# One edit in five parts to a two-layer hybrid trunk: filler and sine tables, first taps, inverse levels, row matmuls, paddings

## The reference

```
proj = hn @ w_in          # gdn qkv, z, beta, a; s5 u; lru x, y; ret q, k, v, g; gates
out_a = gated_deltanet(...)   # width-4 conv on qkv, chunks of 64, unit lower-triangular solve
out_b = s5_layer(...)         # 16 groups, 64 complex states each, diagonal scan
out_c = rg_lru_block(...)     # width-4 conv, gates, linear recurrence
out_d = retention(...)        # rotary q, k, decay, chunks of 128
merged = sum(gates * (branches @ w_branch));  x = x + merged @ w_out
```

## Time and profile before

| | us |
|---|---|
| median of 3 runs | 1408.02 (1407.67 to 1409.34) |
| profiled execution | 1406.48 |
| its span, first to last instruction | 1404.4 |
| TensorE busy | 1349.3 (96%) |
| VectorE busy | 928.1 (66%) |
| ScalarE busy | 645.9 (46%) |
| GpSimd busy | 352.5 (25%) |
| DMA queue's packets | 48.6% of 16 engines |
| mean granted TensorE clock | 0.994 |

### The profile page before, as it was taken

The page is one execution under the profiler, slowest core; times in us unless marked ns, Lnnn a source line. Parts: engine busy times, 40 slices in busy tenths (PEclk is TensorE's granted clock), DMA queues, the critical chain, the costliest instruction groups (busy, mean ns, idle before and its releaser), DMA issues.

```text
span 1404.4 us, 26420 instructions
## 1 busy us (share of the span) xinstructions
PE 1349.3 (96%) x11214; PEld 1317.5 (94%) x11214; DVE 928.1 (66%) x1339; ACT 645.9 (46%) x926; POOL 352.5 (25%) x235
## 2 busy tenths in 40 slices
PE   6999999999999999999999999989989999999998
PEld 6999999888898999999999999989888999999997
DVE  7777446886976855554477765578778677655544
ACT  6444546553234454443464454457332354544432
POOL 2000014355743720000110000235468254100000
PEclk9999999999999999999999999999999999999999
DMA  6555564443232545665555555455422335555553
GB/s 232 185 194 190 168 196 136 136 135 121 61 106 75 181 150 187 194 189 193 186 163 182 184 171 180 156 165 153 131 86 83 104 121 167 161 193 188 175 168 123
DMA packets 61316, 220.17 MB, mean 157 GB/s; under 512 B 6928, under 2 KB 7184, under 8 KB 60688
## 3 DMA queue, kind: packets, MB, share of 16 engines
q1 hardware_dynamic: 61200, 218.50, 48.6%
HBM read 217.42 MB, written 1.05 MB: 156 GB/s over the span
## 4 chain that ended last, share of the span: by engine, by line
PE 76%; DVE 14%; ACT 4%; issue 2%; POOL 2%; DMA 1%; SPq 0%; DVEq 0%; ACTq 0%; POOLq 0%
PE bank L479 23%; PE bank L481 22%; PE bank L480 22%; PE bank L731 2%; DVE wlo L1221 2%; ACT whi L893 1%; DVE qkv L1439 1%; PE bank L499 1%; PE bank L718 1%; DVE tmpA L1455 1%; DVE flat L1241 1%; POOL wlo L1130 1%; DMA raw<-weights 1%; DVE qkv L1437 1%; POOL big L1185 0%
## 5 line engine op out<-in xcount | busy, mean ns | idle before, releaser
L479 PE MATMUL bank<-xh,whi 128*128 128x256 f32 x2384 | 679.6, 285 | 11.4 <-DVE wlo L1221 7.8
L481 PE MATMUL bank<-xh,wlo 128*128 128x256 f32 x2384 | 665.3, 279 | 0.0
L480 PE MATMUL bank<-xl,whi 128*128 128x256 f32 x2384 | 664.7, 279 | 0.0
L1221 DVE TENSOR_TENSOR wlo<-raw,whi 128x1024 fp32r<-128x1024 f32 (+1 forms) x346 | 436.3, 1293 | 168.8 <-ACT whi L893 167.0
L893 ACT ACTIVATE whi<-raw 128x1024 fp32r<-128x1024 f32 (+1 forms) x414 | 415.3, 1036 | 121.4 <-DMA raw<-weights 89.7
L479 PEld LDWEIGHTS bank<-xh,whi 128*128 128x128 f32 x2384 | 449.6, 189 | 17.8 <-issue 8.8
L480 PEld LDWEIGHTS bank<-xl,whi 128*128 128x128 f32 x2384 | 450.6, 189 | 0.3
L481 PEld LDWEIGHTS bank<-xh,wlo 128*128 128x128 f32 x2384 | 450.3, 189 | 0.0
L1130 POOL TENSOR_TENSOR wlo<-raw,whi 128x1024 fp32r<-128x1024 f32 x68 | 172.8, 2553 | 197.2 <-ACT whi L893 197.1
L1171 POOL TENSOR_TENSOR flat<-flat 128x256 f32<-128x256 f32 x36 | 33.6, 933 | 729.7 <-ACT flat L912 728.7
L479 PE MATMUL bank<-hh,whi 128*128 128x256 f32 x704 | 198.9, 283 | 1.5 <-DVE wlo L1221 1.5
(11 more groups left out here) (347 smaller groups left out, 1420.4 us busy)
## 6 DMA issues: line engine op xcount, KB each, us to landing
raw<-weights SPq DMA_DIRECT2D x350, 512.0 KB, 4.0
raw<-weights SPq DMA_DIRECT2D x64, 448.0 KB, 3.9
cst<-consts SPq DMA_DIRECT2D x1, 1088.0 KB, 11.4
par<-params SPq DMA_DIRECT2D x1, 1072.5 KB, 7.7
par<-params SPq DMA_DIRECT2D x1, 1060.5 KB, 9.3
x<-x_in SPq DMA_DIRECT2D x1, 1024.0 KB, 5.4
y_out<-ret SPq DMA_DIRECT2D x4, 256.0 KB, 2.2
ropec<-positions SPq DMA_DIRECT2D x1, 128.0 KB, 2.1
```

The source lines that it names most:

```text
L479: mm(out, w[0], a[0], start=start, stop=False)
L480: mm(out, w[0], a[1], start=False, stop=False)
L481: return mm(out, w[1], a[0], start=False, stop=stop)
L1221: V.tensor_tensor(slot(wlo, i), slot(raw, i), r32(slot(whi, i)), ALU.subtract).then_inc(S("low_dve"), 1)
```

## The change

- The 14 filler matmuls behind the first piece of each down projection are taken out.
- The three table activations now have splits of pieces ahead of them: up to `dn1_0.2` ahead of the sine, up to `dn1_0.4` ahead of Abs, `dn1_0.5` ahead of the cosine.
- Tap 0 of both convolutions is made by ScalarE, 6 and 2 activations of 128x256, tied to VectorE by a new semaphore `taps`. The low parts under `ahead("su")` move from behind the last pass to behind the third.
- In each level of the inverse TensorE's order becomes t0, first half of the gate, xt0, ty0, t1, second half, xt1, ty1; `SIDE` follows, so the side banks are handed out in that order. ScalarE and VectorE make one piece for each pair instead of two ahead of both.
- The row matmuls contract over the 32 partitions that hold the row instead of 128.
- Paddings of 16 and 32 words ahead of `xh` and `xl` move all that lies behind them in SBUF: `xh` and `hh` by 64 bytes, `xl` and `hl` by 192.

```diff
@@ -154,8 +154,7 @@
          ("ktr", "dve"), ("vtr", "dve")]
         + [(n, "dve") for n in ("gb0", "gb1", "kk0", "bb0", "kk1", "bb1", "qk0", "qk1")]
         + [u for lv in range(LEVELS) for u in
-           ([(f"t0_{lv}", "act"), (f"t1_{lv}", "act")]
-            + [(f"{n}{hp}_{lv}", "dve") for hp in range(2) for n in LEVEL_UNITS[lv]]
+           ([u for hp in range(2) for u in [(f"t{hp}_{lv}", "act")] + [(f"{n}{hp}_{lv}", "dve") for n in LEVEL_UNITS[lv]]]
             + [(f"pq{s}", "dve") for s in ([2 * lv, 2 * lv + 1] if lv < 4 else [])]
             + ([("rotq", "dve"), ("rotk", "dve")] if lv == 4 else []))]
         + [("u", "act"), ("w", "act"),
@@ -234,6 +233,7 @@
         whi, wlo = sb("whi", SLOTS * SLOT, F32R), sb("wlo", SLOTS * SLOT, F32R)
         cst = sb("cst", NCST)
         par = sb("par", NPAR)
+        sb("before_xh", 16)
         xh = two("xh", KD, dt=F32R)
         wide = sb("wide", 32 * SEQ)[:].rearrange("p (k t) -> p k t", k=32)
         hh = two("hh", MF, dt=F32R, over="wide")
@@ -252,6 +252,7 @@
         flat8 = two("flat8", 8)
         brh = sb("brh", 8 * SEQ, F32R, over="flat8")[:].rearrange("p (n k t) -> p n k t", n=NB, k=2)
 
+        sb("before_xl", 32)
         xl = two("xl", KD, dt=F32R)
         big = sb("big", 24 * SEQ)
         hl = two("hl", MF, dt=F32R, over="big")
@@ -570,8 +571,6 @@
                             if (j, o, n) == (3, 1, 2):
                                 sum_of_first(which_after)
                             name = f"{unit}.{3 * o + n}"
-                            if (j, o, n) == (0, 0, 1):
-                                keep_busy(14)
                             wh, wl = piece(name)
                             for m in range(k0, k1):
                                 if j == 0 and o == 0:
@@ -641,7 +640,7 @@
             for t in range(2):
                 for hp in range(2):
                     h = 2 * t + hp
-                    last = mm(ps[64 * hp:64 * hp + 64, t * SEQ:(t + 1) * SEQ], ident[:, h:h + 1].to_broadcast([P, 64]), rows, start=True, stop=True)
+                    last = mm(ps[64 * hp:64 * hp + 64, t * SEQ:(t + 1) * SEQ], ident[0:32, h:h + 1].to_broadcast([32, 64]), rows[0:32], start=True, stop=True)
             last.then_inc(S("side"), 1)
             gate(0)
             pe.wait_ge(S("k_normed"), 1)
@@ -656,7 +655,7 @@
                 ps = side_bank(unit)
                 for t in range(2):
                     h = 2 * t + hp
-                    last = mm(ps[:, t * SEQ:(t + 1) * SEQ], ident[:, row + h:row + h + 1].to_broadcast([P, P]), rows, start=True, stop=True)
+                    last = mm(ps[:, t * SEQ:(t + 1) * SEQ], ident[row:row + 32, row + h:row + h + 1].to_broadcast([32, P]), rows[row:row + 32], start=True, stop=True)
                 last.then_inc(S("side"), 1)
 
             def against_k(unit, q0, hp):
@@ -717,8 +716,7 @@
                         else:
                             last = mm(ps[:, i * P:(i + 1) * P], lowc[:, hp, t, j, :], mx[:, hp, t, j, :], start=True, stop=True)
                     last.then_inc(S("side"), 1)
-                gate(4 + lv)
-                for hp in range(2):
+                    half(f"g{4 + lv}", hp)
                     if lv:
                         pe.wait_ge(S("side_act"), side.taken(f"t{hp}_{lv}"))
                     if lv > 1:
@@ -965,10 +963,13 @@
             A(sm["sn"], sm["r1"], ACT.Sin)
             A(sm["cs"], sm["r2"], ACT.Sin).then_inc(S("psin"), 1)
             silus(1, range(4, MF))
+            split_to(piece_at("dn1_0.2") + 1)
             act.wait_ge(S("turns"), 1)
             A(sinE, turns_b, ACT.Sin, scale=SIN_SCALE).then_inc(S("tables"), 1)
+            split_to(piece_at("dn1_0.4") + 1)
             act.wait_ge(S("tables"), 1)
             A(turns_b, turns_b, ACT.Abs).then_inc(S("tables"), 1)
+            split_to(piece_at("dn1_0.5") + 1)
             act.wait_ge(S("tables"), 2)
             A(cosE, turns_b, ACT.Sin, scale=-SIN_SCALE, bias=quarter_col).then_inc(S("tables"), 1)
             squares(0)
@@ -986,10 +987,18 @@
             split_to(piece_at("qkv2.0") + 1)
             A(tmpF[:, 1, :], tmpF[:, 0, :], ACT.Ln, bias=1.0).then_inc(S("ln1p"), 1)
             A(tmpB[:, 1, :], tmpB[:, 0, :], ACT.Tanh, scale=0.5).then_inc(S("ln1p"), 1)
+            def first_taps(i):
+                act.wait_ge(S("main_act"), main.taken(f"qkv{i}"))
+                for t in (2 * i, 2 * i + 1):
+                    last = A(qkv[:, t, :], qkvp[:, t, 0:SEQ], ACT.Identity, scale=par_("gconv", t, t + 1))
+                last.then_inc(S("taps"), 1)
+
             for i in range(3):
                 ahead(f"qkv{i}")
                 act.wait_ge(S("main"), main.ready(f"qkv{i}"))
                 A(qkvp[:, 2 * i:2 * i + 2, 3:], halves(main.bank(f"qkv{i}")[:]), ACT.Identity).then_inc(S("main_act"), 1)
+                if i:
+                    first_taps(i - 1)
             act.wait_ge(S("gc"), 1)
 
             A(tmpF[:, 0, :], tmpC[:, 0, :], ACT.Exp)
@@ -1003,7 +1012,12 @@
                 act.wait_ge(S("main"), main.ready(unit))
                 A(dst, halves(main.bank(unit)[:]), ACT.Identity).then_inc(S("main_act"), 1)
 
+            first_taps(2)
             copied("lx", lxp[:, :, 3:])
+            act.wait_ge(S("main_act"), main.taken("lx"))
+            for t in range(2):
+                last = A(tmpA[:, t, :], lxp[:, t, 0:SEQ], ACT.Identity, scale=par_("lconv", t, t + 1), bias=par_("lcb", t, t + 1))
+            last.then_inc(S("taps"), 1)
             copied("ly", ly)
             copied("su", su)
 
@@ -1070,6 +1084,7 @@
                 for hp in range(2):
                     act.wait_ge(S("side"), side.ready(f"t{hp}_{lv}"))
                     A(flat(mt if lv else mx)[:, hp, :], side.bank(f"t{hp}_{lv}")[:], ACT.Identity).then_inc(S("side_act"), 1)
+                    split_to(last_piece(f"g{4 + lv}") + 2 + hp)
                 gate(4 + lv)
             gate(10)
             act.wait_ge(S("s5gin"), 1)
@@ -1429,30 +1444,26 @@
             ahead("lx")
 
             gw = lambda k, t: par_("gconv", 6 * k + t, 6 * k + t + 1)
-            for k in range(4):
+            for k in range(1, 4):
                 for t in range(6):
-                    if k == 0:
-                        if t % 2 == 0:
-                            dve.wait_ge(S("main_act"), main.taken(f"qkv{t // 2}"))
-                        last = V.tensor_scalar(qkv[:, t, :], qkvp[:, t, 0:SEQ], gw(0, t), None, ALU.mult)
-                    else:
-                        last = V.scalar_tensor_tensor(qkv[:, t, :], qkvp[:, t, k:k + SEQ], gw(k, t), qkv[:, t, :], ALU.mult, ALU.add)
+                    if k == 1 and t % 2 == 0:
+                        dve.wait_ge(S("taps"), t // 2 + 1)
+                    last = V.scalar_tensor_tensor(qkv[:, t, :], qkvp[:, t, k:k + SEQ], gw(k, t), qkv[:, t, :], ALU.mult, ALU.add)
                 if k < 3:
                     link(last)
                 if k == 1:
                     ahead("ly")
+                if k == 2:
+                    ahead("su")
             last.then_inc(S("conv"), 1)
             ahead("su")
 
             xc = tmpA
-            dve.wait_ge(S("main_act"), main.taken("lx"))
+            dve.wait_ge(S("taps"), 4)
             lw = lambda k, t: par_("lconv", 2 * k + t, 2 * k + t + 1)
-            for k in range(4):
+            for k in range(1, 4):
                 for t in range(2):
-                    if k == 0:
-                        last = V.tensor_scalar(xc[:, t, :], lxp[:, t, 0:SEQ], lw(0, t), par_("lcb", t, t + 1), ALU.mult, ALU.add)
-                    else:
-                        last = V.scalar_tensor_tensor(xc[:, t, :], lxp[:, t, k:k + SEQ], lw(k, t), xc[:, t, :], ALU.mult, ALU.add)
+                    last = V.scalar_tensor_tensor(xc[:, t, :], lxp[:, t, k:k + SEQ], lw(k, t), xc[:, t, :], ALU.mult, ALU.add)
                 if k < 3:
                     link(last)
             last.then_inc(S("lru_conv"), 1)
@@ -1573,8 +1584,8 @@
             dve.wait_ge(S("tables"), 2)
             ahead("g3")
             for lv in range(LEVELS):
-                ahead(f"g{4 + lv}")
                 for hp in range(2):
+                    split_to(last_piece(f"g{4 + lv}") + 2 + hp)
                     for n in LEVEL_UNITS[lv]:
                         m = mx if n == "xt" else my
                         unit = f"{n}{hp}_{lv}"
```

## The result

The changed kernel takes **1398.39 us** (median of 4 runs, 1395.42 to 1402.49) beside 1408.05 (1407.67 to 1409.34, 4 runs): ratio 0.9934, 95% interval 0.9914 to 0.9955. It is 9.7 us faster. The forecast was 1383.0 with a range of 1370 to 1395, so the direction was right and the size was off by 15 us. The profiled execution is the slowest of the four, 1402.49 (span 1400.6), which is 4.1 above their median.

A forecast was written before the change was run, and what follows sets the result against it. TensorE, busy 1349 of 1404 us, was taken as the bound, through its matmul stream, stops, filler and half clock. Gains of 14.0 + 7.4 + 1.4 + 2.0 = 24.8 from 1406.5, plus 1.5, gave 1383 us, range 1370 to 1395.

The forecast's parts named there:

- Part 1: Down projections: filler taken out and splits put between the sine tables save 14.0 us; bounds 0 and 14.
- Rival (c): Down projections: tables still delay a piece or TensorE stops at 1.2 GHz, giving 1391 or 1394; chance 0.09.
- Part 2: Convolutions: first taps on ScalarE shrink TensorE's wait and end the slow clock behind it, 3.7 us per layer, 7.4 us.
- Rival (b): Convolutions: gain given back because ScalarE's splits are late by 1.7 and the starving moves to ly: 1391; chance 0.12.
- Part 3: Inverse levels by head pairs: steady levels unchanged, wait for the first inverse goes, 0.7 a layer, 1.4 us.
- Rival (a): Inverse levels: staggering frees them, VectorE's low parts may miss GpSimd, gaining 11.2 us: 1372; chance 0.12.
- Part 4: Row matmuls on 32 partitions: product of the second k hides behind bb0, 1.0 a layer, 2.0 us; bounds 0 and 5.0.
- Part 5: Paddings that move xh, hh, xl and hl in SBUF: taken as 0; far ends ±28 us.
- rival (e): Moved operands: the same address shift makes the matmul cadence faster by 1.2 ns: 1372; chance 0.08.
- Rival (d): Moved xh and xl cost TensorE more per matmul, so slower than before; 1415 at 3.5 ns; chance 0.04.

The follow-up runs named there:

- 64-row trace: The changed kernel with the row products gb and bb on 64 rows instead of 32: 1388.83 us, ratio 0.9872.

## Why the prediction was wrong

**Part 1 (14.0 us) held.** Alone it brought 13.4. The wait in the first feed-forward that the prediction worked out as 0.9 us was 0.73 in the trace before. The schedule that the prediction worked out for ScalarE, splits until 149.5, Abs until 151.4, a split until 152.4, the second sine until 154.4, is the one of the kernel after:

```profile
145.96 1.90 ACT L968 ACTIVATE sinE<-ret 128x2048 f32<-128x2048 f32 x1
147.77 1.88 ACT L891 ACTIVATE whi<-raw 128x1024 fp32r<-128x1024 f32 x2
149.56 1.90 ACT L971 ACTIVATE ret<-ret 128x2048 f32<-128x2048 f32 x1
151.36 0.94 ACT L891 ACTIVATE whi<-raw 128x896 fp32r<-128x896 f32 x1
152.20 2.00 ACT L974 ACTIVATE wide<-ret,small 128x2048 f32<-128x2048 f32 x1
```

Rival (c), stops in place of the filler, did not happen: TensorE doesn't stop for as much as 0.15 us in the down projections.

**Part 2 (7.4 us) failed; it measured 2.0.** The wait ahead of su's piece did go, and there the working was right. The step that failed is "VectorE's work after the convolutions starts about 4 us earlier and TensorE moves up about as much". Most of the 3.74 us of six taps in the earlier trace rows was no work: one tap took 2.50 us, beside a GpSimd low part that ended 0.15 us before it, and the others took 0.34 each. A tap reads one tile, the later passes two, and both kinds were held.

```profile
L1437 DVE TENSOR_SCALAR qkv<-qkvp,par x6: 337/340/2497, 240.5 to 243.9; 128x256 f32<-128x256 f32 x6
```

With the taps gone the hold fell on the next pass, and the later passes, which I left at 2.5 us each, took 4.6 since they now met GpSimd's low parts too. In the run with the taps alone the first pass also begins 1.6 us later (242.03 for 240.46): ScalarE's four taps stand ahead of the split that VectorE's work there begins with. In place of the 4 us the LRU gate matmuls start 1.0 us sooner in layer one (262.96 for 263.96) and 1.9 in layer two. The stop stands ahead of them, with its slow clock in layer one. Rival (b) had the right outcome, that the convolution gain is given back, but by another mechanism: not by late splits of ScalarE.

**Part 3 (1.4 us) held in the trace.** The wait for the first inverse is gone from TensorE's summary, the waits for the scans moved to ty with their size, and the period is 14.6. The 3.4 us measured alone are more, and the distance of its matmuls doesn't explain it (117.04 ns as before, and 117.78 from 719 to 832 us, which costs). The 95% interval of the ratio, 0.9967 to 0.9991, is a gain of 1.3 to 4.6 us, so the forecast lies inside it; whether there are 2 us more, and from what, is open. Rival (a) did not happen.

**Part 4 (2.0 us gained) failed; it cost 7.5 to 9.1.** Its bounds were 0 and 5.0, so a loss was never allowed for. The step that failed is "the product of the second k hides behind bb0: 1.0 saved a layer", together with a cost that the sum put at nothing without a reason: the granted clock of the matmuls around the row products. The row matmuls themselves are as long as on 128 rows: four take 1.12 us, against 1.13 in the earlier trace rows. What they cost lies around them, where 26 matmuls take as long as 50. The stops of 0.8 and 1.4 us at the same place were in the profile before and no slow clock followed them there. The hoped-for overlap of bb0 with the product of the second k did not come either, though they use different rows. The rule that the prediction drew on from the Trainium skill (TensorE: Matmul & The Clock Gate, Part 3), that matmuls on different row groups run at once, agrees with the 64-row trace and not with this pair of 32 and 64 rows.

**Part 5 (0) was near in time and wrong in reason.** The addresses do matter: 117.04 ns became 116.67, a third of the 1.2 ns of rival (e) and in its direction. 2 to 4 us of gain came of it. Rival (d) did not happen.

Put together, from the runs of the parts alone: 0.6 us of the miss comes from part 1, 5.4 from part 2 and 11.1 from part 4, less 2.0 from part 3 and 1.8 from part 5 in the other direction. That is 13.3 of 15 us; the rest is within the scatter of the runs. The range left out the result since neither a clock that falls around short matmuls nor a hold that merely moves on had a place in it.

Left open: what in the chip makes 32 rows lower the clock where 64 don't; why the paddings bring 116.67 ns in place of 117.04, and what brings the stretches of 117.78; and whether the low parts of other stretches would gain as well on VectorE, which wasn't tried.

## What to carry to other kernels

Look at the shortest, median and longest time of an instruction that you mean to remove: if one of six carries the time, look for another engine's instruction beside it. It may be a hold, and here the hold stayed when the instruction went. Where VectorE is the late engine, giving it work that GpSimd does beside it can be a gain: 1.2 us for each low part against 2.15 of hold was worth 8 us here with one line of code. A change that makes TensorE's matmuls smaller must be read with the granted clock of the stretch behind them.

## What was not expected of the hardware

- Row products on 32 rows among 64-row products: two stretches of 6.8 us at 1.2 GHz in layer one, with about the same stops as on 64 or 128 rows, where there are none (1397.35 to 1398.39 us against 1388.20 to 1390.86).
- Two groups of matmuls on 64 different rows each run at once (1.02 us from one to the next but one), a 32-row and a 64-row group on different rows do not (2.14 us).
- Moving operands by 64 and 192 bytes in SBUF changes the distance of two product matmuls at the full clock from 117.04 to 116.67 ns, in every profiled execution. Over 9264 of them that is an estimate of 3.4 us.
- The same matmuls can also run at 117.78 ns for whole feed-forwards. If all of them did, it would be 10 us more than at 116.67, as an estimate.
- A stop of 2.6 us was followed by 1.2 GHz in one kernel and by the full clock in another, at the same place.
